# Band and memory attention: high and low halves of the values in one 128-column stationary operand, the two row halves added on VectorE ahead of the gate

## The chip, the cores and the metric

One core of a Trainium2 chip runs the whole program. The metric is the device time of one execution in microseconds (us). The kernel before took 3130.96 us, the median of three runs (3127.46 to 3132.56).

## What is computed

One inference step of a four-layer encoder over 1024 prompt tokens and 32 decoded tokens that have 512 cached positions. Layers 0 and 3 use band attention (A, 12 heads of 64), layer 1 differential attention (B, 6 heads, values of 128), layer 2 latent attention (C, 12 heads of 64). Every layer also has 4 memory heads (M, 256 memory tokens). Cut to the part that the change touches:

```python
def _band_attend(q, k, v, q_pos, k_pos, rel_bias):
    s = jnp.einsum('bqhd,bkhd->bhqk', q, k) * (A_HEAD_DIM ** -0.5)
    ...
    p = jax.nn.softmax(jnp.where(valid, s + bias, NEG), axis=-1)
    return jnp.einsum('bhqk,bkhd->bqhd', p, v)
...
def _mem_attend(mq, mk, mv):
    p = jax.nn.softmax(jnp.einsum('bqhd,bmhd->bhqm', mq, mk) * (MEM_HEAD_DIM ** -0.5), axis=-1)
    return jnp.einsum('bhqm,bmhd->bqhd', p, mv)
...
        y = jnp.concatenate([br, mo], axis=-1) * jax.nn.silu(gate)
        x = x + y @ w_out[i]
```

## The kernel before

Every large product is made of three TensorE passes over operands that are split into a high half (the rounded fp32r value) and a low half (the rest): high x high, low x high, high x low. TensorE does the projections (`part` items, L1586, 24 matmuls of 352 columns for each third of the tokens), the scores (`S`, L1607), the transposes of the probabilities (`turn`, L1621) and of the values (`vt`, L1633), and probabilities times values (`pv`, L1662), which is summed in PSUM bank `acc[0]`.

Attention goes by **jobs** (two heads, here called lanes), a job by five **units**: four groups of 256 queries in the order g = 1, 2, 0, 3 (0 to 3 for M), and one unit of the 32 decoded queries. A unit's `pv` goes by **chunks** of keys; a chunk has two matmuls of 256 columns (one for each lane), four of 128, or, in the decoded unit, ten (M: four) of 32, and each of them is done in the three passes of `PV_PASSES`. An A job has 12 chunks with 256-wide matmuls (3, 4, 1 and 4 in its four prompt units), an M job has 8. There are 12 A jobs and 8 M jobs: 416 places of a 256-wide matmul, 144 of a 128-wide and 152 of a 32-wide one, each of them three matmuls before.

The order of work on every engine is one list written out in `Plan.unit`. For chunk 0 of a unit it is: transpose the unit's chunk (`turn`); the last `pv` of the unit before; `evac` of that unit; scores of the next unit; `emul` of the unit before (C only); then normalization of the next unit's probabilities (`N`) and projection work for the next job (`part`). So what VectorE does at `evac` stands in its queue ahead of the reduction of the next scores (L1329), which ScalarE's exponentials wait for, and ahead of `N` (L1341 to L1345), which the next unit's first transposes wait for. With one `turn` in flight ahead of each `pv`, VectorE also writes the low half of each transposed chunk (L1358, signal `turned_lo`), ScalarE the high half (L1100, `turned_hi`).

At `evac` of an A or M unit VectorE multiplies the two lanes' rows of `acc[0]` into the gate `y_sb` (L1385, two instructions) and signals `o_read`; `held_free` makes TensorE wait for that before it starts a new sum in `acc[0]`. In the second unit of an A job (called place a below) the next things in VectorE's queue are the scores of unit three, their `N`, a cast of the cached values (L1316), and the low half of a value transpose (L1367), for which TensorE waits before the unit's third transpose. The fourth unit is place c, the decoded unit place d. The last job of a layer has no projection work beside it.

GpSimd makes the low halves of weights (L1412) and operands (L1445), and once, in layer 2, sets the ones that stand beside the values of C (L1426).

Of the kernel before, what the change touches and what calls it, by code (L numbers as in the profile page):

```python
# [10 lines left out]
ALU = mybir.AluOpType  # L11
# [584 lines left out]
def encoder(nc, x_in, mem_in, w8, wc_q, wc_kv, gains_in, lambda_in, rel_in, kcache, vcache, lat_cache,  # L596
# [42 lines left out]
    b_squares = sbuf("b_squares", [2, 256], at=qo_at + 4 * TOK)  # L639
    b_rstd = sbuf("b_rstd", [2, 256], at=qo_at + 4 * TOK + 2048)  # L640
# [25 lines left out]

    v_lo = split_v(v_flat[:, 0:13 * 128])
# [6 lines left out]
    def halves_of_v(kind, rows, block, n):  # L674

        if kind == "B":
            return [split_v(v_flat[0:rows, 128 * (13 * x + block):128 * (13 * x + block + n)]) for x in range(2)]
        return v_hi[0:rows, block:block + n, :, 0:64], v_lo[0:rows, block:block + n]
# [31 lines left out]
    pv_done, o_gated, o_read = signal("pv_done"), signal("o_gated"), signal("o_read")  # L710
# [226 lines left out]
    def scalar_program(act):  # L937
# [67 lines left out]
        for item in plan.order:  # L1005
# [141 lines left out]
            elif name == "evac" and item[1].job.kind == "B":  # L1147
                u = item[1]
                act.wait_ge(*pv_done.upto(u.chunks[-1].p))
                act.activation(b_squares[:, u.n % 2, 0:u.qn], acc[0][:, 0:u.qn],  # L1150
# [21 lines left out]
    def vector_program(dve):  # L1172
# [27 lines left out]
        for item in plan.order:  # L1200
# [168 lines left out]
            elif name == "evac":  # L1369
# [8 lines left out]
                else:  # L1378
                    if u.job.kind == "C":
                        dve.wait_ge(*sums_logged.upto(u.n))  # L1380
                    else:
                        dve.wait_ge(*pv_done.upto(u.chunks[-1].p))
# [3 lines left out]
                    ins.then_inc((o_gated if u.job.kind == "C" else o_read).mark(u.n), 1)  # L1386
# [15 lines left out]
    def pool_program(pool):  # L1402
# [3 lines left out]
        for item in plan.order:  # L1406
# [7 lines left out]
            elif name == "phase":  # L1414
# [8 lines left out]
                elif what == "operands" and more["kind"] == "C":  # L1423
                    pool.wait_ge(*normed_hi.upto(norm_key, KT - 1))
                    pool.wait_ge(*memkv_stored.upto(more["layer"]))
# [34 lines left out]
    def tensor_program(pe):  # L1460
# [4 lines left out]
        def held_free(held):  # L1465
# [3 lines left out]
            elif held is not None:  # L1469
                pe.wait_ge(*(o_gated if held.job.kind == "C" else o_read).upto(held.n))  # L1470
# [37 lines left out]
        for item in plan.order:  # L1508
# [126 lines left out]
            elif name == "pv":  # L1635
# [14 lines left out]
                for y, (vs, ps) in enumerate(PV_PASSES):  # L1650
                    if y == 2:
                        pe.wait_ge(*turned_lo.upto(chunk.a))
                    for i, (lane, block, n, src, dst, w) in enumerate(chunk.mults):
                        if job.kind == "B":
                            rows, values = 128, vb_sp[0:n, vs, block, :]
                        elif vs == 0 and job.kind == "C":
                            rows, values = 128, v_hi[0:n, block, lane, :]
# [147 lines left out]
```

## Time and profile before

| | |
|---|---|
| median of three runs | 3130.96 us |
| profiled execution | 3124.46 us, span 3122.7 us |
| TensorE matmul busy | 2800.3 us, 90% |
| VectorE, ScalarE, GpSimd busy | 41%, 42%, 25% |
| granted TensorE clock, mean | 0.94 of full |
| band attention of layer 0 (290 to 689 us) | TensorE busy 380.7 of 399 us |

Busy TensorE time is a modelled figure, since matmuls overlap. What says more is how far apart a group's matmuls start, and what ended TensorE's idle time ahead of a group.

### The profile page before, as it was taken

The page shows a single profiled execution, that of the slowest core. Times are in us where ns is not written, and L with a number is a line of the kernel's source. Part 1 is how long each engine was busy: PE and PEld are TensorE (multiplying, and loading weights), DVE is VectorE, ACT ScalarE, POOL GpSimd, SP SyncE. Part 2 cuts the span into 40 slices and gives each one's busy share as a digit, 9 for nine tenths or more (in the row PEclk, how much of TensorE's full clock was granted, in tenths as well). Part 3 has the DMA queues.
Part 4 walks back from the last instruction along what each step waited for, and adds up shares of the span by engine and source line. Part 5 has one row for each costly group of instructions (what it writes and reads, how often), then busy time and mean ns, then how long its engine had stood idle before and what let it go on. Part 6 is the DMA issues. An engine that isn't in the chain of part 4 may idle for free.

```text
span 3122.7 us, 46628 instructions
## 1 busy us (share of the span) xinstructions
PE 2800.3 (90%) x18936; PEld 2620.5 (84%) x18936; DVE 1287.2 (41%) x3179; ACT 1316.9 (42%) x2822; POOL 786.6 (25%) x427
## 2 busy tenths in 40 slices
PE   4799999989999999989998678888789989999987
PEld 3788999979988999979987567777689989999887
DVE  3125555561224656661223144444442134555542
ACT  3234444442334555542332235555543244454431
POOL 2222221205422122206421222222116322122212
PEclk8899999989998999989997889899899989999998
DMA  3111111113111111123111000000032111111111
GB/s 121 49 41 54 44 48 49 62 73 131 57 41 58 49 59 56 62 112 97 62 41 35 23 13 9 9 9 7 14 139 90 50 38 52 47 61 47 50 70 69
DMA packets 58197, 171.59 MB, mean 55 GB/s; under 512 B 6720, under 2 KB 15040, under 8 KB 57472
## 3 DMA queue, kind: packets, MB, share of 16 engines
q1 hardware_dynamic: 57984, 168.62, 15.8%
q8 instruction: 150, 2.46, 0.3%
q14 instruction: 63, 0.52, 0.1%
HBM read 134.67 MB, written 33.92 MB: 54 GB/s over the span
## 4 chain that ended last, share of the span: by engine, by line
PE 74%; ACT 11%; DVE 9%; issue 4%; POOL 2%; DMA 0%; SPq 0%; DVEq 0%; ACTq 0%
PE acc L1586 35%; PE acc L1662 10%; PE acc L1549 9%; PE scores L1607 8%; PE turned L1621 6%; ACT prob L1088 4%; PE scores L1503 3%; DVE prob L1329 3%; DVE raw L1219 2%; POOL h_split L1421 2%; PE scores L1481 2%; PE turned L1503 1%; ACT prob L1091 1%; DVE pt_split L1358 1%; ACT pt_split L1100 1%
## 5 line engine op out<-in xcount | busy, mean ns | idle before, releaser
L1586 PE MATMUL acc<-h_split,w_hi 128*128 128x352 f32 (+1 forms) x4860 | 894.6, 330 | 56.0 <-ACT w_rest L959 23.7
L1586 PEld LDWEIGHTS acc<-h_split,w_hi 128*128 128x128 f32 x4860 | 794.3, 192 | 82.2 <-ACT w_rest L959 27.7
L1412 POOL TENSOR_TENSOR w_lo<-w_raw,w_hi 128x1024 fp32r<-128x1024 f32 (+2 forms) x156 | 336.7, 2160 | 1705.1 <-ACT w_hi L1018 1705.1
L1329 DVE CUSTOM_DVE_ANT_0 prob<-scores,bias 128x256 f32<-128x256 f32 (+9 forms) x576 | 337.8, 633 | 523.4 <-PE scores L1607 519.7
L1358 DVE TENSOR_TENSOR pt_split<-turned,pt_split 128x512 fp32r<-128x512 f32 (+4 forms) x564 | 303.4, 553 | 591.0 <-ACT pt_split L1100 590.5
L1662 PE MATMUL acc<-pt_split,v_split 128*64 128x256 f32 (+6 forms) x3486 | 503.3, 281 | 26.2 <-ACT pt_split L1100 8.6
L1586 PE MATMUL acc<-h_split,w_lo 128*128 128x352 f32 (+1 forms) x2430 | 454.4, 324 | 0.0
L1662 PEld LDWEIGHTS acc<-pt_split,v_split 128*64 128x64 f32 (+2 forms) x3486 | 405.5, 161 | 45.6 <-issue 18.3
L1088 ACT ACTIVATE prob<-prob,stat 128x256 f32<-128x256 f32 (+9 forms) x468 | 304.4, 652 | 327.5 <-DVE stat L1329 327.4
L1586 PEld LDWEIGHTS acc<-h_split,w_lo 128*128 128x128 f32 x2430 | 402.6, 190 | 0.0
L1621 PE MATMUL turned<-ident,prob 128*128 128x128 f32 (+2 forms) x1866 | 290.1, 280 | 98.5 <-DVE prob L1345 53.5
L1100 ACT ACTIVATE pt_split<-turned 128x512 fp32r<-128x512 f32 (+4 forms) x564 | 261.5, 482 | 213.3 <-PE turned L1621 212.7
L1621 PEld LDWEIGHTS turned<-ident,prob 128*128 128x128 f32 (+2 forms) x1866 | 217.8, 145 | 139.7 <-DVE prob L1345 64.7
L1607 PE MATMUL scores<-k_split,q_split 64*128 64x512 f32 (+9 forms) x2196 | 301.2, 355 | 27.4 <-DVE stat L1329 18.4
L1018 ACT ACTIVATE w_hi<-w_raw 128x1024 fp32r<-128x1024 f32 (+2 forms) x156 | 150.4, 965 | 344.1 <-PE acc L1549 188.9
L1607 PEld LDWEIGHTS scores<-k_split,q_split 64*128 64x128 f32 (+3 forms) x2196 | 202.9, 194 | 80.3 <-issue 27.5
L1549 PE MATMUL acc<-h_split,w_hi 128*128 128x352 f32 x1152 | 198.1, 324 | 0.0
L1549 PEld LDWEIGHTS acc<-h_split,w_hi 128*128 128x128 f32 x1152 | 188.0, 189 | 0.4
L1298 DVE TENSOR_TENSOR y_sb<-acc,y_sb 128x352 f32<-128x352 f32 x72 | 37.8, 525 | 230.0 <-PE acc L1549 230.0
L972 ACT ACTIVATE raw<-acc 128x352 f32<-128x352 f32 (+1 forms) x132 | 61.6, 467 | 166.2 <-PE acc L1586 165.8
L972 ACT ACTIVATE y_sb<-acc 128x352 f32<-128x352 f32 x72 | 33.6, 467 | 205.9 <-PE acc L1586 205.9
L1503 PE MATMUL scores<-h_split,w_hi 128*128 128x352 f32 x512 | 111.7, 339 | 8.3 <-POOL h_split L1421 4.8
(121 smaller groups left out, 2841.6 us busy)
## 6 DMA issues: line engine op xcount, KB each, us to landing
w_raw<-w SPq DMA_DIRECT2D x132, 512.0 KB, 3.7
x_scr<-y_sb SPq DMA_DIRECT2D x24, 528.0 KB, 5.5
y_sb<-x_scr SPq DMA_DIRECT2D x24, 528.0 KB, 7.8
y_sb<-x_in SPq DMA_DIRECT2D x16, 528.0 KB, 11.5
mw_raw<-w SPq DMA_DIRECT2D x16, 512.0 KB, 7.4
bias<-rel_in SPq DMA_DIRECT2D x24, 320.0 KB, 4.2
raw<-kcache SPq DMA_DIRECT2D x18, 256.0 KB, 4.0
v_cache<-vcache SPq DMA_DIRECT2D x18, 256.0 KB, 4.0
```

The costliest lines, as they stand in the source:

```text
L1018: act.activation(w_hi[:, n % 2, 0:wide], w_raw[:, n % 2, 0:wide], ACT.Copy).then_inc(whi_made.mark(n), 1)
L1088: act.activation(p, p, ACT.Exp, scale=-1.0, bias=stat[0:tile.rows, i:i + 1], accum_out=stat[0:tile.rows, 8 + i:9 + i]).then_inc(exps_ready ...
L1100: ins = act.activation(pt[0:rows, chunk.p % 2, 0, c0:c0 + n], t_ps[chunk.a % 2][0:rows, c0:c0 + n], ACT.Copy)
L1329: dve.tensor_tensor_reduce(out=prob[0:tile.rows, at:at + tile.width], in0=s_ps[lane][0:tile.rows, tile.at:tile.at + tile.width], in1=bias[ ...
L1358: ins = dve.tensor_tensor(pt[0:rows, chunk.p % 2, 1, c0:c0 + n], t_ps[chunk.a % 2][0:rows, c0:c0 + n], pt[0:rows, chunk.p % 2, 0, c0:c0 + ...
L1412: pool.tensor_tensor(w_lo[:, n % 2, 0:wide], w_raw[:, n % 2, 0:wide], w_hi[:, n % 2, 0:wide].bitcast(F32), ALU.subtract).then_inc(wlo_made ...
L1503: ins = pe.matmul(pair_banks[3 * i + c][:, 0:n], (w_hi, w_lo)[ws][:, w % 2, 128 * k:128 * k + 128], x[:, xs, k, a:a + n], start=k == ks[0] ...
L1549: ins = pe.matmul(acc[i % 2][:, 0:n], (w_hi, w_lo)[ws][:, w % 2, 128 * k:128 * k + 128], h_v[:, xs, k, a:a + n], start=k == 0 and y == 0, ...
L1586: ins = pe.matmul(acc[s.bank][:, 0:s.cols], w[ws][:, 128 * k:128 * k + 128], x(xs, k), start=k == 0 and y == 0, stop=k == s.k_tiles - 1 an ...
L1607: ins = pe.matmul(s_ps[lane][0:tile.rows, tile.at + col:tile.at + col + n], q[rows, qs, tile.q0:tile.q0 + tile.rows], k[rows, ks, key:key ...
L1621: ins = pe.transpose(t_ps[chunk.a % 2][0:n, to:to + rows], prob[0:rows, at:at + n], ident[0:rows, 0:rows])
L1662: ins = pe.matmul(acc[0][0:rows, dst:dst + w], values, pt[0:n, chunk.p % 2, ps, src:src + w], start=c == 0 and i == 0 and y == 0, stop=las ...
```

## The change

The values' low halves of A and M jobs no longer lie in `v_lo`, but in columns 64 to 127 beside the high halves (`v_hi`). The first pass loads all 128 columns, so that rows 0 to 63 of `acc[0]` get high x high and rows 64 to 127 low x high; the second pass is gone. The third (high values, low probabilities) writes rows 0 to 63 as before. In a unit's last chunk the last matmul of the first pass is issued at the end. VectorE copies rows 64 to 127 to a new buffer `o_sum` (signal `o_half`), adds rows 0 to 63 (signal `o_gated`, for which TensorE now waits), and multiplies into the gate later, at `emul`. The ones of C are set after layer 2's memory jobs.

```diff
+    o_sum = sbuf("o_sum", [2, 512], at=qo_at + 4 * TOK)
...
+        if kind in "AM":
+            return v_hi[0:rows, block:block + n, :, 0:64], v_hi[0:rows, block:block + n, :, 64:128]
...
+                if u.before.job.kind == "M":
+                    act.wait_ge(*o_read.upto(u.before.n))
                 act.activation(b_squares[:, u.n % 2, 0:u.qn], acc[0][:, 0:u.qn],
...
-                else:
-                    if u.job.kind == "C":
-                        dve.wait_ge(*sums_logged.upto(u.n))
-                    else:
-                        dve.wait_ge(*pv_done.upto(u.chunks[-1].p))
+                elif u.job.kind == "C":
+                    dve.wait_ge(*sums_logged.upto(u.n))
                     for lane in range(2):
                         gate = y_sb[64 * lane:64 * lane + 64, u.job.tile, q]
                         ins = dve.tensor_tensor(gate, acc[0][0:64, 256 * lane:256 * lane + u.qn], gate, ALU.mult)
-                    ins.then_inc((o_gated if u.job.kind == "C" else o_read).mark(u.n), 1)
+                    ins.then_inc(o_gated.mark(u.n), 1)
+                else:
+                    both = lambda x: x.rearrange("p (l q) -> p l q", l=2)[:, :, 0:u.qn]
+                    dve.wait_ge(*pv_done.upto(u.chunks[-1].p))
+                    if u.before is not None and u.before.before is not None:
+                        dve.wait_ge(*o_read.upto(u.before.before.n))
+                    dve.tensor_copy(both(o_sum[0:64, u.n % 2, :]), both(acc[0][64:128, :])).then_inc(o_half.mark(u.n), 1)
+                    dve.wait_ge(*o_half.upto(u.n))
+                    dve.tensor_tensor(both(o_sum[0:64, u.n % 2, :]), both(acc[0][0:64, :]), both(o_sum[0:64, u.n % 2, :]),
+                                      ALU.add).then_inc(o_gated.mark(u.n), 1)
+            elif name == "emul" and item[1].job.kind in "AM":
+                u = item[1]
+                dve.wait_ge(*o_gated.upto(u.n))
+                for lane in range(2):
+                    gate = y_sb[64 * lane:64 * lane + 64, u.job.tile, u.q0:u.q0 + u.qn]
+                    ins = dve.tensor_tensor(gate, o_sum[0:64, u.n % 2, 256 * lane:256 * lane + u.qn], gate, ALU.mult)
+                ins.then_inc(o_read.mark(u.n), 1)
...
-                elif what == "operands" and more["kind"] == "C":
-                    pool.wait_ge(*normed_hi.upto(norm_key, KT - 1))
-                    pool.wait_ge(*memkv_stored.upto(more["layer"]))
+                elif what == "latents":
+                    pool.wait_ge(*pv_done.upto(more["before"]["unit"].chunks[-1].p))
                     pool.memset(v_hi[:, :, :, 64:128].bitcast(F32), 1.0).then_inc(ones_set.mark("values"), 1)
...
-                pe.wait_ge(*(o_gated if held.job.kind == "C" else o_read).upto(held.n))
+                pe.wait_ge(*(o_read if held.job.kind == "B" else o_gated).upto(held.n))
...
+                if job.kind in "AM":
+                    listed = [(0, i) for i in range(final + 1)] + [(2, i) for i in range(final + 1)]
+                    if last:
+                        listed = listed[:final] + listed[final + 1:] + [(0, final)]
...
+                    elif vs == 0 and (job.kind == "C" or ps == 0):
+                        rows, values = 128, v_hi[0:n, block, lane, :]
+                    elif vs == 0:
+                        rows, values = 64, v_hi[0:n, block, lane, 0:64]
```

TensorE, fourth unit of layer 0's first A job: two chunks of `pv`, the second of them the unit's last. Before:

```order
L1662 MATMUL acc<-pt_split,v_split 64x256 [waits turned_hi]
L1662 MATMUL acc<-pt_split,v_split 64x256 x3
L1662 MATMUL acc<-pt_split,v_split 64x256 [waits turned_lo]
L1662 MATMUL acc<-pt_split,v_split 64x256
L1586 MATMUL acc<-h_split,w_lo 128x352 x8
L1621 MATMUL turned<-ident,prob 128x32 [waits turned_lo,probs_ready]
L1621 MATMUL turned<-ident,prob 128x32 x7
L1621 MATMUL turned<-ident,prob 32x32 x2
L1662 MATMUL acc<-pt_split,v_split 64x128 [waits turned_hi]
L1662 MATMUL acc<-pt_split,v_split 64x128 x7
L1662 MATMUL acc<-pt_split,v_split 64x128 [waits turned_lo]
L1662 MATMUL acc<-pt_split,v_split 64x128 x3
```

The same place after the change:

```order
L1691 MATMUL acc<-pt_split,v_split 128x256 [waits turned_hi]
L1691 MATMUL acc<-pt_split,v_split 128x256
L1691 MATMUL acc<-pt_split,v_split 64x256 [waits turned_lo]
L1691 MATMUL acc<-pt_split,v_split 64x256
L1605 MATMUL acc<-h_split,w_lo 128x352 x8
L1640 MATMUL turned<-ident,prob 128x32 [waits turned_lo,probs_ready]
L1640 MATMUL turned<-ident,prob 128x32 x7
L1640 MATMUL turned<-ident,prob 32x32 x2
L1691 MATMUL acc<-pt_split,v_split 128x128 [waits turned_hi]
L1691 MATMUL acc<-pt_split,v_split 128x128 x2
L1691 MATMUL acc<-pt_split,v_split 64x128 [waits turned_lo]
L1691 MATMUL acc<-pt_split,v_split 64x128 x3
```

Two matmuls instead of four stand ahead of the wait for the low half in a usual chunk.

VectorE, place a (second unit of an A job), from the release of the first unit's `acc[0]` on. Before:

```order
L1385 TENSOR_TENSOR y_sb<-acc,y_sb 64x256 [waits pv_done,side_read]
L1385 TENSOR_TENSOR y_sb<-acc,y_sb 64x256
L1329 ISA prob,stat<-scores,bias 128x128 [waits scores_ready,turned]
...
L1329 ISA prob,stat<-scores,bias 128x256
L1329 ISA stat 128x1
L1341 RECIPROCAL stat<-stat 128x2 [waits exps_ready]
L1344 TENSOR_SCALAR prob<-prob,stat 128x128 [waits recips_ready]
L1345 TENSOR_SCALAR prob<-prob,stat 128x128
L1316 CAST v_split<-v_cache 128x8x64 [waits pv_done,vcache_loaded]
L1367 TENSOR_TENSOR v_split<-turned,v_split 32x128 [waits turned_hi]
```

After:

```order
L1396 COPY o_sum<-acc 64x512 [waits o_read,pv_done,side_read]
L1398 TENSOR_TENSOR o_sum<-acc,o_sum 64x512 [waits o_half]
L1336 ISA prob,stat<-scores,bias 128x128 [waits scores_ready,turned]
...
L1405 TENSOR_TENSOR y_sb<-o_sum,y_sb 64x256 [waits o_gated]
L1405 TENSOR_TENSOR y_sb<-o_sum,y_sb 64x256
L1348 RECIPROCAL stat<-stat 128x2 [waits exps_ready]
L1351 TENSOR_SCALAR prob<-prob,stat 128x128 [waits recips_ready]
L1352 TENSOR_SCALAR prob<-prob,stat 128x128
L1323 CAST v_split<-v_cache 128x8x64 [waits pv_done,vcache_loaded]
L1374 TENSOR_TENSOR v_split<-turned,v_split 32x2x64 [waits turned_hi]
```

A copy and an addition of 512 elements now stand ahead of the score reductions, and the two gate multiplications between these and the normalization.

## Rows read from the trace of the kernel before

**Rows 1.** The page: the span.

```profile
span 3122.7 us, 46628 instructions
```

**Rows 2.** Stretches: us; PE, PEld, DVE, ACT, POOL busy; PEclk; DMA share; GB/s.

```profile
290.00:689.00 399.00, 380.68 (x2941) 353.15 (x2939) 219.30 (x597) 196.55 (x447) 81.93 (x45) 0.96 0.13 45
1604.00:1690.00 86.00, 63.41 (x405) 55.59 (x405) 46.27 (x166) 35.50 (x102) 8.58 (x5) 0.76 0.10 32
456.20:523.10 66.90, 65.73 (x518) 61.63 (x518) 36.17 (x99) 32.54 (x76) 14.76 (x9) 1.00 0.16 51
519.40:523.10 3.70, 2.97 (x23) 2.61 (x21) 3.38 (x16) 2.40 (x10) 0.39 (x1) 1.00 0.02 4
671.90:675.30 3.40, 3.40 (x24) 2.47 (x25) 1.59 (x4) 0.60 (x1) 0.00 (x0) 0.53 0.00 0
```

**Rows 3.** Waits of PE: the first from 200 to 290 us, the others 290 to 689.

```profile
PE turned L1621 <- DVE prob L1345: 9.0, 4, 3.0
...
PE turned L1621 <- DVE v_split L1367: 5.4, 6, 1.8
PE turned L1621 <- DVE prob L1345: 4.0, 2, 2.9
```

**Rows 4.** Timeline, PV groups: start, busy us, engine, line, op, form, count.

```profile
1625.62 0.60 PE L1662 MATMUL acc<-pt_split,v_split 128*64 128x256 f32 x3
1625.62 0.95 PE L1662 MATMUL acc<-pt_split,v_split 128*64 128x256 f32 x6
1060.23 0.95 PE L1662 MATMUL acc<-pt_split,v_split 128*128 128x256 f32 x6
343.52 0.60 PE L1662 MATMUL acc<-pt_split,v_split 128*64 128x128 f32 x6
1871.15 0.76 PE L1662 MATMUL acc<-pt_split,v_split 128*128 128x128 f32 x6
```

**Rows 5.** Groups by line and form on VectorE: busy us, mean ns, idle before.

```profile
L1358 DVE TENSOR_TENSOR pt_split<-turned,pt_split 128x512 fp32r<-128x512 f32 x364 | 250.7, 689 | 443.1 <-ACT pt_split L1100 442.9
L1385 DVE TENSOR_TENSOR y_sb<-acc,y_sb 64x256 f32<-64x256 f32 x208 | 86.0, 413 | 9.8 <-ACT recip L1143 5.8 <-PE acc L1662 2.4
L1392 DVE TENSOR_TENSOR y_sb<-y_sb,recip 128x256 f32<-128x256 f32 x24 | 10.2, 425 | 0.0
L1316 DVE CAST v_split<-v_cache 128x512 fp32r<-128x512 f32 x18 | 7.6, 420 | 0.0
```

**Rows 6.** Timeline at place a of the fourth A job of layer 0.

```profile
519.49 0.84 DVE L1385 TENSOR_TENSOR y_sb<-acc,y_sb 64x256 f32<-64x256 f32 x2
522.75 0.28 DVE L1367 TENSOR_TENSOR v_split<-turned,v_split 32x128 fp32r<-32x128 f32 x1
523.09 0.66 PE L1621 MATMUL turned<-ident,prob 128*128 128x128 f32 x4 [0.73 <-DVE v_split L1367]
```

**Rows 7.** Timeline at places c (to 552.63) and d of that job.

```profile
551.33 0.15 DVE L1341 RECIPROCAL stat<-stat 32x2 f32<-32x2 f32 x1 [1.00 <-ACT prob L1088]
552.35 0.67 DVE L1358 TENSOR_TENSOR pt_split<-turned,pt_split 128x512 fp32r<-128x512 f32 x1
552.63 0.94 PE L1662 MATMUL acc<-pt_split,v_split 128*64 128x256 f32 x6
561.42 0.83 DVE L1385 TENSOR_TENSOR y_sb<-acc,y_sb 64x256 f32<-64x256 f32 x2
565.65 0.17 DVE L1341 RECIPROCAL stat<-stat 128x2 f32<-128x2 f32 x1 [0.23 <-ACT prob L1088]
566.25 0.48 DVE L1345 TENSOR_SCALAR prob<-prob,stat 128x512 f32<-128x512 f32 x1
566.79 0.66 PE L1621 MATMUL turned<-ident,prob 128*128 128x128 f32 x4
```

**Rows 8.** Timeline: a two-operand VectorE instruction in SBUF, and GpSimd in layer 2.

```profile
1052.70 1.93 DVE L1398 TENSOR_TENSOR y_sb<-y_sb,b_rstd 128x256 f32<-128x256 f32 x1 [5.36 <-ACT b_rstd L1158]
1699.65 2.38 POOL L1412 TENSOR_TENSOR w_lo<-w_raw,w_hi 128x1024 fp32r<-128x1024 f32 x1 [54.21 <-ACT w_hi L1018]
```

More of the change, by code:

```diff
@@ L709, in encoder @@
     turned, turned_hi, turned_lo = signal("turned"), signal("turned_hi"), signal("turned_lo")
-    pv_done, o_gated, o_read = signal("pv_done"), signal("o_gated"), signal("o_read")
+    pv_done, o_half, o_gated, o_read = signal("pv_done"), signal("o_half"), signal("o_gated"), signal("o_read")
     scores_ready, scores_biased = signal("scores_ready"), signal("scores_biased")
@@ L1649, in tensor_program @@
                         pe.wait_ge(*ones_set.upto("values"))
-                for y, (vs, ps) in enumerate(PV_PASSES):
-                    if y == 2:
-                        pe.wait_ge(*turned_lo.upto(chunk.a))
[L1653 to L1657, printed above, removed]
-                        elif vs == 0:
-                            rows, values = 64, v_hi[0:n, block, lane, 0:64]
-                        else:
-                            rows, values = 64, v_lo[0:n, block, lane, :]
-                        ins = pe.matmul(acc[0][0:rows, dst:dst + w], values,
-                                        pt[0:n, chunk.p % 2, ps, src:src + w],
-                                        start=c == 0 and i == 0 and y == 0,
-                                        stop=last and i == len(chunk.mults) - 1 and y == 2)
+                final = len(chunk.mults) - 1
@@ new lines, in tensor_program @@
+                if job.kind in "AM":
+                    listed = [(0, i) for i in range(final + 1)] + [(2, i) for i in range(final + 1)]
+                    if last:
+                        listed = listed[:final] + listed[final + 1:] + [(0, final)]
+                else:
+                    listed = [(y, i) for y in range(3) for i in range(final + 1)]
+                lo_awaited = False
+                for y, i in listed:
+                    vs, ps = PV_PASSES[y]
+                    lane, block, n, src, dst, w = chunk.mults[i]
+                    if ps == 1 and not lo_awaited:
+                        pe.wait_ge(*turned_lo.upto(chunk.a))
+                        lo_awaited = True
+                    if job.kind == "B":
+                        rows, values = 128, vb_sp[0:n, vs, block, :]
+                    elif vs == 0 and (job.kind == "C" or ps == 0):
+                        rows, values = 128, v_hi[0:n, block, lane, :]
+                    elif vs == 0:
+                        rows, values = 64, v_hi[0:n, block, lane, 0:64]
+                    else:
+                        rows, values = 64, v_lo[0:n, block, lane, :]
+                    ins = pe.matmul(acc[0][0:rows, dst:dst + w], values,
+                                    pt[0:n, chunk.p % 2, ps, src:src + w],
+                                    start=c == 0 and i == 0 and y == 0,
+                                    stop=last and (y, i) == listed[-1])
```

## The prediction

> **What bounds the kernel now.** I read the stretches first. In the band attention of layer 0 TensorE's matmuls are busy 380.7 of 399 us, and in one usual A job, a period of 66.9 us, 65.7 us at the full clock [rows 2]. VectorE is busy in little over half of that job (36.2 us). So TensorE bounds these stretches, and less work on it should show. The table of waits then says where TensorE is not the limit: six times, once for each A job of the layer, it waits for the low half of a value transpose on VectorE, 5.4 us in total, and in the memory jobs four times for VectorE's normalization, 9.0 us in total [rows 3]. Layer 2's memory jobs, without projection work in the second of them, have TensorE busy 63.4 of 86 us [rows 2]. The timeline of one job shows how near VectorE is at the other places: it is busy 3.38 of the 3.7 us ahead of place a [rows 2], and at place d TensorE starts the next job's transposes at 566.79 us, 0.06 us after VectorE's normalization ended at 566.73 [rows 7]. That is a tie, so whatever makes VectorE later there makes TensorE later by as much.
>
> **What the change removes.** The price of a matmul is how much longer a group is busy with three more of them. A 256-wide one costs (0.95 - 0.60) / 3 = 0.117 us, and with 128 columns loaded a group of six takes 0.95 us as well [rows 4]: the wider load is free behind 256 columns. The removed 256-wide passes are worth 416 x 0.117 = 48.7 us. A 128-wide one starts every 0.06 us or so behind 64 loaded columns; the group of six in layer 2 of which four load 128 columns takes 0.76 us instead of 0.60 [rows 4], so that each wide load adds 0.04 us, and the removed pass is given back but for some 0.02 us. With the 32-wide ones, which I take alike, these are 3 to 5 us. Some of the matmuls run at half clock, where they cost near twice as much; that adds 3 us. TensorE has 55 us less to do, 3.0 us in a usual A job (12 x 2 x 0.117 = 2.8, and 0.2).
>
> **What it adds on VectorE.** Before, a prompt unit's `evac` was two multiplications of 413 ns, 0.83 us. Now it is a copy and an addition of 64 x 512, and the multiplications follow at `emul`. The addition is like L1358, 512 elements with one operand in PSUM: 0.69 us. Both operands of the multiplications are in SBUF; L1392 has 0.425 us for that, so they stay at 0.84 us. The copy is in no row. Its bounds are 0.42 us, the cast of 512 elements within SBUF, and 0.69 us, the instruction with two operands, one of them in PSUM [rows 5]. I take 0.65 us, since the source is PSUM as in the second row. Here a rule speaks against the change: the Trainium skill ("VectorE: DVE Perf Modes", section "Why PSUM operands drop a tier") says that an fp32 operand in PSUM keeps VectorE at one element a cycle. By the cast's row the copy would run at about two, and the sum below would come out 11 us lower; by the rule it does not. No run here shows a copy from PSUM yet, and the sum stands on the bounds above.
>
> So `acc[0]` is released 0.65 + 0.69 - 0.83 = 0.5 us later (0.53 with a handover), the next scores' reduction and ScalarE's exponentials come 0.53 us later, and what stands behind `emul` up to 1.36 us later. That is 1.36 us more of VectorE for each of 80 prompt units, 109 us in all. None of it costs anything where VectorE idles.
>
> **The places of a usual A job**, one after the other, and the saving that is lost there because TensorE arrives earlier only to wait:
>
> - Place a. VectorE has nearly no gap from `evac` at 519.49 to the low half of the value transpose at 522.75, for which TensorE already waits 0.73 us [rows 6]. Nothing absorbs the 1.36 us but some 0.06. The third transposes start 1.3 us later than now, and the saving of two chunks ahead of them (0.47 us) is lost.
> - Place c. VectorE idles 1.00 us ahead of the decoded unit's normalization, waiting for the exponentials [rows 7]. The multiplications go there; the 0.53 us of the exponentials remains. It moves the low half that ends at 553.02. TensorE is to use it behind four matmuls of the group that starts at 552.63, at about 553.2: 0.15 us of slack, now with two matmuls ahead instead of four. So +0.5 us, and 0.47 us of saving lost.
> - Place d. `evac` at 561.42, then scores and normalization without a gap but 0.23 us before the second [rows 7]. 1.36 - 0.23 = 1.1 us later, and TensorE, tied to it, waits for all of it.
> - The first, third and the rest of the second and fourth unit keep their savings, but for one chunk (0.24 us) that I take as lost in the first unit, behind a value transpose.
>
> The job: -3.0 + (1.3 + 0.47) + (0.5 + 0.47) + 1.1 + 0.24 = +1.1 us. Ten such jobs: +11 us. The last A job of layers 0 and 3 has no projection work; the longest waits of the row with six (1.8 us) and of the one with two (2.9 us) are its [rows 3]. Savings count little where the chain transpose, halves, `pv` sets the pace, and the three places cost 2.9 us: I take +2.5 us each, +5.
>
> **The memory jobs.** Their 64 wide chunks save 64 x 0.234 = 15 us of work, but the four waits of [rows 3] show the chain evac, scores, exponentials, normalization, transposes as the limit. In the two memory jobs of a layer I count five units tied to it, two of them at about 0.5 us, three at 0.7 to 1.1: +3.9 us, against 1.9 us that the others keep: +2 us in each of three layers. In layer 2 all ten units are chain-bound: +3.5 us. Together +9.5 us.
>
> **The clock.** After a 2.9 us wait for normalization the stretch from 671.9 us runs at 0.53 [rows 2, 3], near 1.2 GHz instead of 2.4. At place a the wait goes from 0.73 to about 2.5 us, at place d from nothing to 1.1 us. If three of the ten jobs in question get such a stretch, as long as that row's, it costs half the row's 3.4 us where TensorE is the limit: +5 us.
>
> **Parts that I cost at nothing.** The ones of C are set at the start of the latents; GpSimd's next work there comes after 54.2 us of idleness, at 1699.65 [rows 8], some 15 us after layer 2's memory jobs end; without that cover the fill would cost its own 1 to 2 us. ScalarE's new wait ahead of the first B unit is for multiplications issued a unit earlier. The order of DMAs doesn't change.
>
> **The sum.** 11 + 5 + 9.5 + 5 = +30 us on the profiled execution's 3124.5 us (span 3122.7 [rows 1]), 3154.5 us. The median before is 6.5 us above that execution: 3161 us.
>
> **Rivals.**
> - Faster, by a smaller lateness. A usual A job breaks even when the three places come to 3.0 - 0.47 - 0.47 - 0.24 = 1.8 us instead of 2.9, 0.6 us each. That takes a copy of 0.42 us and multiplications that find a gap everywhere: then it is about 0.3 us a place, the job -0.9 us, and with the memory jobs at -5 the kernel is some 16 us faster: 3115 us. For it speaks VectorE's 30 us of idleness in the job; against it, that the places have almost none. In the extreme, where all 55 us count, 3076 us. Chance 0.18.
> - No difference: the terms nearly cancel, because the lateness at c or at a is caught up, 3131 us. Chance 0.12.
> - Slower by the clock. TensorE's new waits bring a stretch at half clock into nearly every A job and lengthen those in the memory jobs: 12 more of them are 20 us on top, 3181 us. For it speaks the row at 0.53; against it, that the present 1.8 us wait at place a is followed by no such row that I could find. Chance 0.12.
> - Slower by GpSimd. An instruction with two operands in SBUF, 0.42 us alone, took 1.93 us beside a GpSimd subtraction [rows 8], and the gate multiplications become of that kind. With 1.5 us in 20 units, 3191 us. In the A job GpSimd's subtractions lie a few us away from the new `emul`, so chance 0.05.
> - My forecast, 0.53.
>
> **Range and chances.** Fine effects under 0.2% (6.3 us) can't be told from no change here. The likeliest case alone holds 3140 to 3178 us: the copy's lower bound gives 3150, no clock term 3156, twice the memory term and clock term 3176. Holding 8 in 10, the range reaches from 3114 to 3190 us. Faster 0.18, same 0.12, slower 0.70.
>
> **What would show it.** Right: 256-wide groups of four matmuls (0.71 us busy); a copy of 0.6 to 0.7 us; TensorE's wait at place a about 2.5 us and a new one of about 1.1 us at place d in nearly each A job; the period of a usual A job near 68 us; VectorE's busy time up by about 110 us and TensorE's down by some 50. Wrong: the wait at a under 1.3 us, none at d, or gate multiplications of over 1 us. The forecast fails if VectorE's additional work starts earlier than I think, with the shorter `pv`, since I hold its start at `evac` as tied to the transposes and not to `pv`.

## The result: 3167 us, 1.2% slower

The changed kernel takes 3167.34 us (median of four runs, 3166.04 to 3168.66), the kernel before 3130.34 us beside it (3127.46 to 3132.56): 1.0124 times the time before, 95% interval 1.0109 to 1.0138. The prediction said 3161 us in a range of 3114 to 3190, and slower with 0.70. The profiled execution took 3166.04 us. Three executions in a slow state are left out of the medians: one of the variant pe_alone below (7610 us) and two of the kernel before (7190 and 3805 us).

The page of the changed kernel, its span, busy times and the chain of waits by engine:

```profile
span 3164.3 us, 45404 instructions
...
PE 2789.6 (88%) x18224; PEld 2602.0 (82%) x18224; DVE 1399.9 (44%) x3379; ACT 1314.2 (42%) x2822; POOL 786.4 (25%) x427
...
PE 67%; DVE 15%; ACT 10%; issue 5%; POOL 2%; DMA 0%; SPq 0%; DVEq 0%; ACTq 0%
```

TensorE has 712 matmuls fewer (18,936 before) and is busy only 11 us less. Its share of the chain that ended last went from 74% to 67%, VectorE's from 9% to 15%.

Groups by line and form on VectorE (busy us, mean ns | idle before), which answer to [rows 5]:

```profile
L1405 DVE TENSOR_TENSOR y_sb<-o_sum,y_sb 64x256 f32<-64x256 f32 x160 | 66.7, 417 | 1.2
L1396 DVE COPY o_sum<-acc 64x512 f32<-64x512 f32 x80 | 55.5, 693 | 3.5 <-PE acc L1691 0.6 <-issue 0.2
L1398 DVE TENSOR_TENSOR o_sum<-acc,o_sum 64x512 f32<-64x512 f32 x80 | 54.6, 683 | 2.7
```

The copy costs 693 ns, as much as an instruction with two operands. The multiplications, now with both operands in SBUF, cost 417 ns; no GpSimd instruction holds them here.

Waits of TensorE from 301 to 700 us, the band attention of layer 0 (us in total, times, longest), which answer to [rows 3]:

```profile
PE turned L1640 <- DVE prob L1352: 11.5, 7, 3.2
PE turned L1640 <- DVE v_split L1374: 10.8, 7, 2.4
```

4.0 us in two waits for normalization became 11.5 us in seven; five of the seven are the new waits at place d. 5.4 us in six waits for the value's low half became 10.8 us in seven: place a.

The timeline of layer 3's third A job, from the low half ahead of `evac` to place a, then place d (start, busy us; in brackets the idle time before and what ended it):

```profile
2801.83 0.69 DVE L1365 TENSOR_TENSOR pt_split<-turned,pt_split 128x512 fp32r<-128x512 f32 x1 [2.51 <-ACT pt_split L1105]
...
2802.55 0.69 DVE L1396 COPY o_sum<-acc 64x512 f32<-64x512 f32 x1
...
2803.28 0.68 DVE L1398 TENSOR_TENSOR o_sum<-acc,o_sum 64x512 f32<-64x512 f32 x1
...
2804.07 0.71 PE L1691 MATMUL acc<-pt_split,v_split 128*128 128x256 f32 x4 [0.34 <-issue]
...
2804.99 0.85 DVE L1405 TENSOR_TENSOR y_sb<-o_sum,y_sb 64x256 f32<-64x256 f32 x2
...
2807.14 0.66 PE L1640 MATMUL turned<-ident,prob 128*128 128x128 f32 x4 [1.57 <-DVE v_split L1374]
...
2851.23 0.66 PE L1640 MATMUL turned<-ident,prob 128*128 128x128 f32 x4 [1.18 <-DVE prob L1352]
```

VectorE has no gap from 2801.83 to the low half at 2807.08. TensorE's wait at place a is 1.57 us (0.73 before, [rows 6]), and there is a second one that the prediction did not list: the second unit's first group starts at 2804.07, right behind the addition that releases `acc[0]` at 2803.96. The row calls it "issue"; four matmuls that are ready, and an addition that ends 0.11 us ahead of them, say what it is. At place d there are 1.18 us where there were none [rows 7].

Windows (columns as in [rows 2]): five usual A jobs of layer 0, two single jobs of layer 3, and 6.8 us near the start of a job of layer 0.

```profile
301.30:647.00 345.70, 324.95 (x2343) 300.82 (x2343) 209.46 (x545) 161.93 (x375) 73.39 (x40) 0.97 0.15 48
2783.60:2851.20 67.60, 63.41 (x471) 58.70 (x471) 41.82 (x109) 32.33 (x76) 14.71 (x8) 1.00 0.15 50
2713.00:2783.60 70.60, 66.39 (x472) 61.34 (x472) 41.91 (x109) 32.47 (x76) 14.71 (x8) 0.95 0.15 48
442.00:448.80 6.80, 6.80 (x31) 6.10 (x30) 3.00 (x9) 2.21 (x5) 0.36 (x1) 0.50 0.37 117
```

The two single jobs have the same instructions and waits. The second holds 6.8 us at a granted clock of 0.50, near 1.2 GHz, the first none, and that is the 3 us between them. So a usual A job has two numbers: its time at full clock, from one first transpose to the next, and how many half-clock stretches of 3.4 us it holds. They all begin within 4 us of a job's start, behind place d and in the decoded unit's small matmuls. Each adds 1.4 us; a stretch of 6.8 us counts as two. Counted from the granted clock over time in each profile, for the ten usual A jobs:

| kernel | median us | A job at full clock | wait at a | wait at d | half-clock stretches |
|---|---|---|---|---|---|
| before | 3130 | 66.9 | 0.73 | 0.03 | 2 |
| changed | 3167 | 67.7 | 1.57 | 1.18 | 11 |
| pe_alone | 3094 | 65.1 | 1.01 | 0.06 | 2 |
| dve_alone | 3173 | 69.2 | 1.39 | 1.03 | 5 |
| late_mult | 3158 | 68.1 | 1.02 | 0.61 | 7 |
| act_copy | 3121 | 66.1 | 1.38 | 0.90 | 9 |
| act_pool | 3121 | 66.2 | 1.23 | 0.62 | 7 |
| act_one | 3123 | 66.2 | 1.23 | 0.64 | 7 |
| mid_add | 3118 | 66.3 | 0.71 | 0.81 | 7 |
| before_mid | 3145 | 68.1 | 0.32 | 0.67 | 10 |
| m_only | 3142 | 66.9 | 0.73 | 0.03 | 10 |
| fill_d | 3153 | 67.7 | 1.57 | 0.20 | 2 |
| act_fill | 3121 | 66.1 | 1.38 | 0.09 | 3 |

In a_only every usual job but the first of a layer holds a stretch; it has ten. Jobs 0 of layers 0 and 3 follow memory jobs and are 1.3 to 1.5 us shorter than the rest at full clock.

The counts are of one execution each, and they change from execution to execution. The kernel before, run 57 times beside the experiments, took 3119.9 us at a mean granted clock of 0.943 and 3135.05 us at 0.937. Its profiled execution lies 2 to 6 us under its medians, which at 1.4 us each is some two to four stretches; those of fill_d and dve_alone lie 6.6 and 5.3 us under theirs, that of before_mid 7.3 us above. The times at full clock and the waits repeat within about 0.1 us from job to job and don't share this doubt.

### The profile page after: what moved, and what is told of

It reads as the page before. It is cut to its first block, busy times and chain, and to the rows that moved or that the text cites. A ratio compares the mean times of both kernels' runs of the same rounds, so it can differ in the third digit from the quotient of the medians.

```text
span 3164.3 us, 45404 instructions
## 1 busy us (share of the span) xinstructions
PE 2789.6 (88%) x18224; PEld 2602.0 (82%) x18224; DVE 1399.9 (44%) x3379; ACT 1314.2 (42%) x2822; POOL 786.4 (25%) x427
## 4 chain that ended last, share of the span: by engine, by line
PE 67%; DVE 15%; ACT 10%; issue 5%; POOL 2%; DMA 0%; SPq 0%; DVEq 0%; ACTq 0%
PE acc L1605 32%; PE acc L1568 9%; PE acc L1691 8%; PE scores L1626 6%; PE turned L1640 5%; DVE prob L1336 4%; PE scores L1522 3%; ACT prob L1093 2%; DVE raw L1226 2%; POOL h_split L1441 2%; ACT pt_split L1105 2%; DVE pt_split L1365 2%; PE scores L1500 2%; PE turned L1522 1%; ACT prob L1096 1%
## 5 line engine op out<-in xcount | busy, mean ns | idle before, releaser
L1605 PE MATMUL acc<-h_split,w_hi 128*128 128x352 f32 (+1 forms) x4860 | 909.8, 334 | 55.8 <-ACT w_rest L964 23.4
L1605 PEld LDWEIGHTS acc<-h_split,w_hi 128*128 128x128 f32 x4860 | 808.3, 195 | 82.9 <-ACT w_rest L964 27.3
L1691 PE MATMUL acc<-pt_split,v_split 128*128 128x256 f32 (+7 forms) x2774 | 455.8, 295 | 39.8 <-issue 13.8
L1691 PEld LDWEIGHTS acc<-pt_split,v_split 128*128 128x128 f32 (+3 forms) x2774 | 357.4, 183 | 65.4 <-issue 29.2
L1568 PEld LDWEIGHTS acc<-h_split,w_hi 128*128 128x128 f32 x1152 | 188.0, 189 | 0.4
```

What stands on the lines that cost most here:

```text
L1568: ins = pe.matmul(acc[i % 2][:, 0:n], (w_hi, w_lo)[ws][:, w % 2, 128 * k:128 * k + 128], h_v[:, xs, k, a:a + n], start=k == 0 and y == 0, ...
L1605: ins = pe.matmul(acc[s.bank][:, 0:s.cols], w[ws][:, 128 * k:128 * k + 128], x(xs, k), start=k == 0 and y == 0, stop=k == s.k_tiles - 1 an ...
L1691: ins = pe.matmul(acc[0][0:rows, dst:dst + w], values, pt[0:n, chunk.p % 2, ps, src:src + w], start=c == 0 and i == 0 and y == 0, stop=las ...
```

## The experiments

My theory after the result: VectorE's longer queue ahead of places a, c and d costs more than TensorE saves, and TensorE's waits bring half-clock stretches. Rivals: the removed matmuls were worth little; the memory jobs carry the loss; the clock falls for another reason.

**Each half alone.** pe_alone keeps TensorE's new passes and gives VectorE its old work, the multiplications at `evac`; dve_alone keeps VectorE's new work and gives TensorE its three passes (its copy takes rows 0 to 63, so the outputs of these jobs are doubled). pe_alone:

```diff
+                    for lane in range(2):
+                        gate = y_sb[64 * lane:64 * lane + 64, u.job.tile, q]
+                        ins = dve.tensor_tensor(gate, acc[0][0:64, 256 * lane:256 * lane + u.qn], gate, ALU.mult)
```

dve_alone:

```diff
-                if job.kind in "AM":
-                    listed = [(0, i) for i in range(final + 1)] + [(2, i) for i in range(final + 1)]
```

> TensorE has the new two passes, and VectorE does what it did before (two gate multiplications of 0.41 us from rows 0 to 63 of the sum bank, no copy, no addition). The part low values x high probabilities is left out of the output. Theory (VectorE's lateness at the three places and the clock eat the saving): without the added VectorE work the places keep their timing of before, so the 55 us less of TensorE work show almost whole: 3130 - 55 = 3075 us, somewhat more (3085) if the waits at the ties a and d grow because TensorE arrives earlier, with the wait at place a near 1.2 us. Rival (the removed matmuls were worth little, or wider loads cost something that I did not see): 3120 us or more. A rival on the clock (less dense TensorE work brings the half clock even without later VectorE work): 3100 us, with a mean granted clock of 0.93 or less.

> TensorE has its three passes as before, and VectorE has the copy, the addition and the later multiplications of the change (the copy takes rows 0 to 63, so that the attention output of these jobs is doubled). Theory: the kernel changed and this one differ by the TensorE work that still counts there. In a usual A job the changed kernel is 0.75 us longer than before; 3.0 us of TensorE work are back, of which about 1.2 us were hidden at places a and c, so a usual job is some 2.5 us longer than before, in all 3130 + 55 to 70 = 3185 to 3200 us. Rival (VectorE's lateness costs little and it is the new TensorE order, two matmuls ahead of the wait for the low half, that costs): 3150 us or less.

Measured: pe_alone 3094.0 us against 3129.6 beside it (ratio 0.9894, 0.9875 to 0.9913), dve_alone 3173.05 us (1.0145, 1.0129 to 1.0161). TensorE's half alone gains 36 us by the medians (33 by the ratio), not 45 to 55. VectorE's half alone costs 43 us, less than I had expected (55 to 70), so that the two kernels with VectorE's work differ by only 6 us. The five jobs of layer 0 in before, pe_alone and dve_alone:

```profile
299.20:635.00 335.80, 330.28 (x2567) 309.75 (x2567) 180.99 (x495) 161.90 (x374) 73.92 (x40) 0.99 0.15 51
```

```profile
297.40:623.00 325.60, 316.21 (x2344) 293.73 (x2344) 180.90 (x495) 161.13 (x375) 73.80 (x40) 0.99 0.16 52
```

```profile
302.70:651.60 348.90, 333.78 (x2567) 310.63 (x2567) 207.22 (x545) 162.80 (x375) 73.53 (x40) 0.99 0.15 48
```

At full clock the halves nearly add up: -1.8 us a job for TensorE's, +2.3 for VectorE's, and +0.8 for both. What does not add up is the clock: 0.99 in these three rows and 0.97 in the changed kernel's; 2, 2 and 5 stretches against 11. In these two executions the changed kernel has six stretches more than dve_alone, 8 us, which take back half of what TensorE saves beside VectorE's new work (1.6 us in each of ten jobs).

**The multiplications later, the copy elsewhere.**

late_mult, in `Plan.unit`:

```diff
-                if prev is not None:
+                if prev is not None and prev.job.kind not in "AM":
                     order.append(("emul", prev))
...
+                if c == 1 and prev is not None and prev.job.kind in "AM":
+                    order.append(("emul", prev))
```

act_copy, in ScalarE's program at `evac`:

```diff
+                act.activation(both(o_sum[0:64, u.n % 2, :]), both(acc[0][64:128, :]), ACT.Copy).then_inc(o_half.mark(u.n), 1)
```

> The changed kernel, with the two gate multiplications (0.83 us) moved in VectorE's order from ahead of the next unit's normalization to behind it. Theory (VectorE's queue ahead of the transposes is what is late): at places a and d TensorE starts 0.8 us earlier; place c, where the multiplications lay in an idle gap, is unchanged. 20 to 22 such places in A jobs, and half of the memory units: 3167 - 18 - 5 = 3145 us, 3140 if some of the half-clock stretches go as well. The waits of TensorE's transposes for the normalization and the value's low half fall from 79 + 21 us to about 75. Rival (the copy and addition ahead of the scores are what counts, since exponentials follow from them; the multiplications find a gap): 3160 us or more.

> The changed kernel, with the copy of rows 64 to 127 done by ScalarE instead of VectorE (VectorE's addition waits for it). Theory: VectorE's queue is shorter by 0.69 us in each of 80 units, but the sum bank and the scores' reduction stay as late, since a copy on ScalarE takes as long (0.6 to 0.8 us with its handover). At place a, where VectorE works without a gap, the wait for the copy takes the place of the copy, so there is no gain if ScalarE copies at the same moment; gains come only where VectorE had other work to finish at that moment. So 3155 to 3167 us. Rival (the copy on VectorE is the cost itself, and ScalarE's is hidden): 0.7 us at places a, c and d, 3167 - 25 = 3142 us. Rival (ScalarE's exponentials and halves fall behind): 3175 us.

Measured: late_mult 3158.2 us (ratio 1.0100, 1.0083 to 1.0117), 9 us less than the changed kernel instead of 22; act_copy 3121.0 us (0.9976, 0.9966 to 0.9986), 46 us less where I had allowed 12. Both forecasts missed.

late_mult at place c of the same job:

```profile
2831.82 1.27 POOL L1468 TENSOR_TENSOR q_split<-q_raw,q_split 128x512 fp32r<-128x512 f32 x1 [3.51 <-ACT q_split L1130]
2832.40 2.41 DVE L1409 TENSOR_TENSOR y_sb<-o_sum,y_sb 64x256 f32<-64x256 f32 x2
...
2833.06 1.46 POOL L1468 TENSOR_TENSOR k_split<-raw,k_split 128x512 fp32r<-128x512 f32 x1
...
2835.58 0.45 PE L1695 MATMUL acc<-pt_split,v_split 128*64 128x256 f32 x2 [0.66 <-DVE pt_split L1369]
```

The waits at a and d fell by 0.55 and 0.57 us, less than the 0.8 us of the theory, and the multiplications now stand among the low halves, beside GpSimd's subtractions: two of them take 2.41 us instead of 0.85, and TensorE waits 0.66 us for the low half behind them. A job is 0.4 us longer at full clock than in the changed kernel; only fewer stretches and the memory jobs gained. The Trainium skill ("SBUF — State Buffer", section "SBUF: two separate sides") says that a VectorE instruction with two inputs in SBUF and a GpSimd instruction that reads SBUF lock each other out for the whole instruction; the row agrees, and GpSimd's subtraction beside it took 1.46 us instead of 1.27.

act_copy, the same stretch as above ahead of place a:

```profile
2764.61 0.59 ACT L1158 ACTIVATE o_sum<-acc 64x512 f32<-64x512 f32 x1
2764.61 0.69 DVE L1372 TENSOR_TENSOR pt_split<-turned,pt_split 128x512 fp32r<-128x512 f32 x1 [2.50 <-ACT pt_split L1105]
...
2765.30 0.68 DVE L1401 TENSOR_TENSOR o_sum<-acc,o_sum 64x512 f32<-64x512 f32 x1
...
2766.26 0.71 PE L1694 MATMUL acc<-pt_split,v_split 128*128 128x256 f32 x4
...
2769.16 0.65 PE L1643 MATMUL turned<-ident,prob 128*128 128x128 f32 x4 [1.38 <-DVE v_split L1381]
```

This is what I had called the only way to a gain and thought rare: when the sum is complete, VectorE is busy with the low half of the chunk already transposed, 0.69 us, and ScalarE copies in that time. It is so at a and at c in every job. The copy disappears, the addition ends 1.37 us behind the low half's start instead of 2.13, and the group at 2766.26 no longer waits. Of the 43 us between the two profiles, 20 lie in the ten usual A jobs (16 of them at full clock); the rest lies in the memory jobs, the last A job of each layer and layer 1.

**The multiplications off VectorE, or halved.** act_pool adds per lane into 128 partitions and lets GpSimd multiply; act_one does the same with the multiplication on VectorE.

```diff
+                    for lane in range(2):
+                        ins = dve.tensor_tensor(o_sum[64 * lane:64 * lane + 64, u.n % 2, 0:u.qn],
+                                                acc[0][0:64, 256 * lane:256 * lane + u.qn],
+                                                o_sum[0:64, u.n % 2, 256 * lane:256 * lane + u.qn], ALU.add)
...
+                pool.tensor_tensor(gate, o_sum[:, u.n % 2, 0:u.qn], gate, ALU.mult).then_inc(o_multiplied.mark(u.n), 1)
```

> As the kernel with the copy on ScalarE, and also the gate multiplication taken from VectorE: VectorE's addition is done in two halves of 256 elements (0.83 us together) that put the second lane on partitions 64 to 127, and GpSimd multiplies 128x256 into the gate (0.74 us, by its 128x256 rows). VectorE then has 0.83 us a unit, what it had before the change. Theory (the order on VectorE ahead of normalization and transposes is the whole cost, TensorE's saving is real): the usual A job comes to the 65.1 us of the kernel with TensorE's change alone, and the whole to 3095 to 3102 us. Rival (a VectorE instruction with two operands in SBUF is held while GpSimd works, so that GpSimd's 80 multiplications slow VectorE's subtractions and additions): 3110 us or more. Rival (GpSimd's subtractions of 2.4 us ahead of the multiplication hold up the next release of the sum buffer): waits of ScalarE's copy for the multiplication show, and the time is over 3121 us.

> As the kernel with the copy on ScalarE, with the addition in two halves on VectorE (0.83 us instead of 0.68) and one gate multiplication of 128x256 on VectorE (0.42 us instead of 0.85). Theory: VectorE is 0.28 us shorter ahead of the normalization at places a and d, 0.14 us longer ahead of the exponentials. 0.28 us in 20 places less 0.14 in the ten at c: 3121 - 4 = 3117 us. Rival (the exponentials are the tie, not VectorE's queue): 3123 us.

Measured: act_pool 3121.2 us (ratio 0.9980, 0.9972 to 0.9989), act_one 3122.98 us (0.9987, 0.9978 to 0.9995). Both 66.2 us a job. Whether VectorE multiplies or not makes no difference any more: in act_pool at place d it idles for ScalarE's exponentials ahead of the second normalization, and TensorE still waits 0.62 us.

```profile
2880.51 0.17 DVE L1357 RECIPROCAL stat<-stat 128x2 f32<-128x2 f32 x1 [0.22 <-ACT prob L1095]
...
2881.65 0.66 PE L1646 MATMUL turned<-ident,prob 128*128 128x128 f32 x4 [0.62 <-DVE prob L1361]
```

act_pool's forecast of 65.1 us failed. Its two rivals had named times that fit, but not for their reasons: VectorE's subtractions and additions keep their 689 and 417 ns beside GpSimd's multiplications, and ScalarE's copy never waits for one. The queue on VectorE was the cost only as far as it was longer than the exponentials. What is left against pe_alone at place d (0.6 us) lies ahead of the reductions: copy and additions take 1.4 us, the two multiplications 0.83.

**Behind the first reductions.** mid_add moves act_one's addition there, before_mid the multiplications of the kernel before.

```diff
                     self.scores(nxt, 0)
+                if prev is not None:
+                    order.append(("add", prev))
                 if narrow:
                     self.scores(nxt, 1)
```

> As the kernel with the copy on ScalarE, halves added and one multiplication (3123 us), with VectorE's addition moved from ahead of the next unit's first score reduction to behind it. Two kernels with and without the multiplication on VectorE took the same 66.2 us for a usual A job, 1.1 us above the one with TensorE's change alone, so that the multiplication is no longer what counts. Theory: what is left is the chain copy on ScalarE, addition on VectorE, score reduction, exponentials, which the addition leaves now: place d loses its wait of 0.6 us and place a some 0.2 us, the usual A job comes to 65.3 us, and the whole to 3123 - 9 - 3 (memory jobs) = 3111 us, 3105 if half-clock stretches go with it. Rival (the sum bank is released later, and the first group of probabilities times values of the second unit waits for it): 66 us or more, 3120 us.

> The kernel before, with its two gate multiplications (0.83 us) moved behind the next unit's first score reduction; TensorE's work is that of before. It says how much of a gain of the reordered kernel comes from the order alone. Theory: at place d TensorE now arrives with VectorE, so there is nothing to win there, and at place a VectorE's queue has no gap, so that its order does not matter: 3120 to 3130 us, only the memory jobs gain some. Rival: the chain of the exponentials limits here too, and it gains as much as the other: 3115 us or less.

Measured: mid_add 3118.12 us (ratio 0.9967, 0.9956 to 0.9978), the lowest median of the kernels that leave nothing out, under both the kernel before and the changed one; before_mid 3145.07 us (1.0054, 1.0040 to 1.0068), 18 us slower than before, outside both forecasts. Its places c and d:

```profile
625.36 0.84 DVE L1387 TENSOR_TENSOR y_sb<-acc,y_sb 64x256 f32<-64x256 f32 x2
626.35 0.89 PE L1664 MATMUL acc<-pt_split,v_split 128*64 128x256 f32 x6 [0.57 <-DVE y_sb L1387]
...
638.87 0.56 DVE L1331 CUSTOM_DVE_ANT_0 prob<-scores,bias 128x384 f32<-128x384 f32 x1 [0.67 <-PE scores L1609]
...
644.13 0.66 PE L1623 MATMUL turned<-ident,prob 128*128 128x128 f32 x4 [0.67 <-DVE prob L1347]
```

The move helps at a (0.32 us of wait) and hurts at c, where the bank is released late, and at d, where VectorE now idles 0.67 us for TensorE's scores: the multiplications had lain in that time and cost nothing. The same trade keeps mid_add's job at 66.3 us.

**Which jobs.** a_only and m_only make the change for one kind of job (`job.kind in "A"`, `in "M"`).

> The change for the band jobs (A) alone; the memory jobs (M) are as before. Theory: the A jobs bring +29 us (ten usual ones +21, of which 13 from longer half-clock stretches, the last ones of layers 0 and 3 +8), the memory jobs +8: this kernel takes 3155 to 3162 us. Rival (the memory jobs, bound by the chain through VectorE, carry most of the loss): 3145 us or less.

> The change for the memory jobs (M) alone; the band jobs are as before. Theory: +8 us, 3136 to 3142 us. By the prediction's term it is +9.5 us, 3140 us. Rival: 3150 us or more, if the memory jobs carry most of the loss.

Measured: a_only 3152.94 us (1.0081, 1.0065 to 1.0096), +26 us; m_only 3142.40 us (1.0048, 1.0033 to 1.0063), +15 to 16 us. That is more than the memory jobs' own time: its five A jobs of layer 0, with the instructions of before, took 341.3 us instead of 335.8.

```profile
299.90:641.20 341.30, 336.34 (x2563) 315.67 (x2563) 181.70 (x497) 161.33 (x373) 73.61 (x40) 0.97 0.15 49
2765.70:2832.60 66.90, 65.72 (x519) 61.60 (x518) 36.17 (x99) 32.53 (x75) 14.76 (x8) 1.00 0.16 51
```

At full clock such a job is the 66.9 us of before, with a wait of 0.03 us at d. Yet there are ten half-clock stretches instead of two. So half of my theory falls: TensorE's new waits are not needed for a stretch. Inside these jobs nothing differs but the time at which they start, so a shift in time seems to be enough; four jobs in a row got theirs 3.8 us behind the start. No run makes such a shift by itself.

**Work in the wait.** fill_d is the changed kernel, with six matmuls issued twice ahead of place d; act_fill adds five to act_copy. The product is started anew behind them.

```diff
+                if s.what == "v" and parts == 1 and s.job.kind == "A":
+                    for k in range(6):
+                        pe.matmul(acc[s.bank][:, 0:s.cols], w[0][:, 128 * k:128 * k + 128], x(0, k),
+                                  start=k == 0, stop=k == 6 - 1)
```

> The changed kernel (3167 us), with six matmuls of the last third of the v projection issued twice, 1.1 us of TensorE work in each A job, right ahead of place d where TensorE waits 1.2 us for normalization. Theory on the clock (the half-clock stretches at the start of an A job come from TensorE's wait and the small matmuls of the decoded unit behind it): the work goes into the wait, costs nothing at full clock (67.7 us), and most of the 14 half-clock stretches that I count in the ten usual A jobs go: 14 x 1.4 = 20 us less at most, 3150 to 3158 us. Rival (the clock falls for another reason, and the wait does not matter): 3167 us or more, with as many stretches.

> The kernel with the copy on ScalarE (3121 us), with five matmuls of the last third of the v projection issued twice in each A job, 0.9 us of TensorE work ahead of place d, where it waits 0.9 us. This joins the two edits that gained, the copy off VectorE and the filled wait. In that kernel's ten usual A jobs I count nine half-clock stretches; the filled one kept 2 of 11. Seven or eight of them gone at 1.4 us each, and full-clock jobs unchanged at 66.1 us: 3121 - 11 = 3110 us. Rival (the stretches come from something else in the two kernels, or the work doesn't fit the wait): 3120 us or more.

The 14 stretches in fill_d's expectation are a miscount: the changed kernel has 11. Measured: fill_d 3152.68 us (1.0078, 1.0065 to 1.0090), 15 us less than the changed kernel, with 0.9 us more of busy matmuls in each A job (1.1 expected). Place d, and the five jobs of layer 0 with one of them:

```profile
572.64 0.66 PE L1644 MATMUL turned<-ident,prob 128*128 128x128 f32 x4 [0.20 <-DVE prob L1352]
```

```profile
303.30:641.70 338.40, 322.07 (x2373) 298.42 (x2373) 209.15 (x545) 160.44 (x375) 73.73 (x40) 0.99 0.16 50
505.00:572.60 67.60, 64.35 (x477) 59.65 (x477) 41.81 (x109) 32.23 (x76) 14.74 (x8) 1.00 0.16 50
```

A full-clock job is 67.6 us as before the filling, with 64.35 us of matmuls instead of 63.41, and two stretches are left of eleven in the profiled execution, the fastest of its five. act_fill: 3121.35 us (0.9974, 0.9963 to 0.9986), no gain over act_copy's 3121.0, against a forecast of 3110. Its stretches went from nine to three and the ten jobs came down by 8 us in the profile; the last memory jobs ahead of the A jobs, which have the doubled matmuls and no such wait, lost 3.3 us, and the rest was lost in layer 1 and at its end.

## Why the prediction was right

The sum was +30 us; the profiled executions differ by 41.6 us, the medians by 37.0. The prediction set the median 6.5 us above its profiled execution; for the changed kernel it is 1.3 us, which brings the two closer. The size is in part owed to terms that cancel: the usual A jobs at full clock were put 3 us too high, the clock 10 us and the last A jobs 3 us too low.

- **The removed work.** Put at 55 us, 3.0 us in a usual A job. In pe_alone, which has the saving without the lateness, the matmuls of such a job at full clock are busy 2.6 us less (65.8 to 63.1 us), so the term was 0.4 us too large; the job is 1.8 us shorter, and the rest goes into longer waits. Groups of four take 0.71 us, as forecast.
- **The copy, the addition, the multiplications.** 693, 683 and 417 ns against 650, 690 and 425. The copy's upper bound was the right one, and the cast within SBUF [rows 5] would have been the wrong row. The Trainium skill ("VectorE: DVE Perf Modes", section "Why PSUM operands drop a tier") holds an fp32 operand in PSUM to one element a cycle; the trace agrees, with 693 ns for the copy from PSUM against 420 for the cast within SBUF. VectorE's busy time rose by 113 us (110 forecast).
- **Places.** Against pe_alone the lateness that TensorE sees is 0.9 us past place a, 0.6 at c and 1.1 at d: 2.6 us in all, 2.9 forecast (1.3, 0.5, 1.1). Place a is the term that was too large. The forecast let all but 0.06 us of VectorE's 1.36 us pass through. From the start of the low half ahead of `evac` to the end of the value's low half VectorE takes 4.15 us before (518.88 to 523.03, the row below and [rows 6]) and 5.25 us after (2801.83 to 2807.08), 1.1 us more: VectorE had small gaps there, ahead of the reciprocal and of the value's low half, that took up the rest. The chunks behind the wait caught up another 0.2 us. The wait itself came to 1.57 us and not to about 2.5, also because TensorE, held 0.34 us for `acc[0]`, arrived there later than forecast. A usual job is therefore +0.8 us instead of +1.1, ten of them +8.

```profile
518.88 0.69 DVE L1358 TENSOR_TENSOR pt_split<-turned,pt_split 128x512 fp32r<-128x512 f32 x1 [2.74 <-ACT pt_split L1100]
```

- **The last A jobs.** +5 forecast; +3.2 us from layer 0's to the next layer's first transposes and +4.9 from layer 3's to the end, the layers' ends and their half-clock stretches among it.
- **Memory jobs.** +9.5 forecast, +7.8 in the profile.
- **The clock.** The term that fell furthest short. Three stretches of 1.7 us were forecast, +5; nine more came in the usual A jobs at 1.4 us, +12.6, and two more, 2.9 us, in the B jobs of layer 1, where nothing was changed. The case "slower by the clock" named the effect and gave it 0.12. The reason that it gave, longer waits, is at best a part: m_only has the stretches without the waits.
- TensorE's busy time fell by 11 us and not by 50, since a matmul at half clock counts double. The mean granted clock of 0.929 instead of 0.94 makes some 449 us at half clock instead of 375 (twice the missing share of the span); half of these 74 us, 37, is added busy time, and that is by this estimate most of the gap between 50 and 11.

The rival "faster, by a smaller lateness" was wrong for this kernel and right for its neighbours: with the copy on ScalarE the A job is 0.8 us shorter than before, as that rival's -0.9 us had it. It needed another engine, not a cheaper copy.

Open: what decides which job gets a half-clock stretch. More TensorE work ahead of place d took most of them away in two kernels, and in m_only, where only the time of the jobs' start differs, there were eight more; no run fixed the shift and varied only the work. The two stretches of the kernel before are a low count: its profiled execution is 5.9 us under the median beside the changed kernel, and the changed kernel's 1.3 us, so the profiles overstate the loss (41.6 us) against the medians (37.0 us) by 4.6 us.

## What to carry to other kernels

When work moves from the busiest engine to one with idle time, ask where in the second engine's queue it lands: the same copy of 0.7 us, taken to ScalarE, made the kernel 46 us faster, since in most units ScalarE was free just while VectorE worked on the low half ahead of it. An instruction that looks as if it stood in the way may lie in time that costs nothing (`evac` beside the making of the scores); moving it can lose more than adding to it. Where TensorE's clock has stretches at half speed, count them apart from the time at full clock, in more than one execution, before explaining a difference of under 1%: identical jobs differed by 1.4 us for each.

## What was not expected of the hardware

- Ten half-clock stretches in m_only's unchanged A jobs instead of two in one execution each, with waits no longer than before: 11 us of 3142 that no instruction of these jobs explains.
- Six redundant matmuls in a wait made a kernel 15 us faster.
- Two SBUF multiplications of 64x256 beside GpSimd's subtractions took 2.41 us instead of 0.85, and 0.85 a few us earlier in the order.
